# Up products of two feed-forwards as seven block products of 256 tokens in place of eight

## The reference, cut to what matters

```python
# block 1
h = rms_norm(x, ffn_norm)
act = jax.nn.silu(h @ w_gate) * (h @ w_up)
x = x + act @ w_down
# block 2
gate, val = jnp.split(h @ w_up, 2, axis=-1)
x = x + (jax.nn.silu(causal_dwconv(gate, conv_w)) * val) @ w_down
```

## Time and profile before

| | us |
|---|---|
| median of 3 runs | 1906.7 |
| profiled execution | 1906.78 |
| its span in the trace | 1904.9 |
| TensorE busy | 1827.2 |
| VectorE busy | 662.6 |
| ScalarE busy | 698.9 |
| GpSimd busy | 829.2 |

### The profile page before, as it was taken

How to read it: one execution, slowest core, us unless ns; L and a number is a source line. 1 busy time by engine, 2 the same in 40 slices (tenths; PEclk the granted TensorE clock), 3 DMA queues, 4 the chain that set the end, 5 groups by cost and what they waited for, 6 DMA issues and landing times. The chain is left out here.

```text
span 1904.9 us, 23268 instructions
## 1 busy us (share of the span) xinstructions
PE 1827.2 (96%) x9070; PEld 1517.7 (80%) x9070; DVE 662.6 (35%) x1110; ACT 698.9 (37%) x1355; POOL 829.2 (44%) x537
## 2 busy tenths in 40 slices
PE   6999999999999999999989989999998999999998
PEld 5998776778877888888768978887887878888886
DVE  2443333351433110011038438983204233303322
ACT  3233344232333232222236228873423333313322
POOL 2444222234442444444336428982651244444442
PEclk9999999999999999999989989999999999999999
DMA  6232111212352323332324320003441223233331
GB/s 219 78 89 62 47 48 51 56 53 80 98 177 71 95 94 94 100 100 93 107 71 136 102 62 28 1 1 100 133 133 34 67 82 106 90 96 92 104 107 45
DMA packets 222876, 161.87 MB, mean 85 GB/s; under 512 B 9768, under 2 KB 197296, under 8 KB 222768
## 3 DMA queue, kind: packets, MB, share of 16 engines
q1 hardware_dynamic: 221712, 159.32, 28.2%
q10 hardware_dynamic: 1056, 1.06, 0.2%
HBM read 156.15 MB, written 2.11 MB: 83 GB/s over the span
## 5 line engine op out<-in xcount | busy, mean ns | idle before, releaser
L306 POOL TENSOR_TENSOR w_low<-ring,w_high 128x1024 fp32r<-128x1024 f32 (+2 forms) x303 | 682.1, 2257 | 935.6 <-ACT w_high L298 935.6
L319 PE MATMUL psum<-hT,w_high 128*128 128x512 f32 x1232 | 491.8, 399 | 9.8 <-PEq L183 6.1
L321 PE MATMUL psum<-hT,w_low 128*128 128x512 f32 x1232 | 485.0, 394 | 0.0
L320 PE MATMUL psum<-hL,w_high 128*128 128x512 f32 x1232 | 484.9, 394 | 0.0
L298 ACT ACTIVATE w_high<-ring 128x1024 fp32r<-128x1024 f32 (+2 forms) x303 | 296.8, 981 | 507.9 <-PE psum L321 507.8
L319 PEld LDWEIGHTS psum<-hT,w_high 128*128 128x128 f32 x1232 | 235.0, 191 | 63.5 <-issue 11.6
L321 PEld LDWEIGHTS psum<-hT,w_low 128*128 128x128 f32 x1232 | 234.2, 190 | 50.5
L320 PEld LDWEIGHTS psum<-hL,w_high 128*128 128x128 f32 x1232 | 234.9, 191 | 47.1
L319 PE MATMUL psum<-w_high,hT 128*128 128x512 f32 (+2 forms) x384 | 132.9, 346 | 7.2 <-POOL w_low L306 3.3
L319 PE MATMUL psum<-w_high,ffn_act 128*128 128x512 f32 x352 | 139.1, 395 | 0.0
L320 PE MATMUL psum<-w_low,ffn_act 128*128 128x512 f32 x352 | 138.9, 395 | 0.0
(11 more groups left out here) (363 smaller groups left out, 2564.1 us busy)
## 6 DMA issues: line engine op xcount, KB each, us to landing
ring<-in_w_in SPq DMA_DIRECT2D x58, 512.0 KB, 3.8
ring<-in_ffn_w_up SPq DMA_DIRECT2D x44, 512.0 KB, 3.8
ring<-in_w_gate SPq DMA_DIRECT2D x22, 512.0 KB, 3.8
ring<-in_w_up SPq DMA_DIRECT2D x22, 512.0 KB, 3.9
ring<-in_w_down SPq DMA_DIRECT2D x20, 512.0 KB, 3.6
ring<-in_ffn_w_down SPq DMA_DIRECT2D x20, 512.0 KB, 3.7
ring<-in_nsa_w_in SPq DMA_DIRECT2D x18, 512.0 KB, 3.8
ring<-in_ca_wkv SPq DMA_DIRECT2D x16, 512.0 KB, 3.8
```

Source lines behind the costliest of these rows:

```text
L306: nc.gpsimd.tensor_tensor(tile_view(w_low, n, SPLIT), tile_view(ring, n, RING), tile_view(w_high, n, SPLIT), ALU.subtract).then_inc(w_lo, 1)
L319: nc.tensor.matmul(ps, lhsT=sh, rhs=mh, start=first, stop=False)
L320: nc.tensor.matmul(ps, lhsT=sh, rhs=ml_, start=False, stop=False)
L321: return nc.tensor.matmul(ps, lhsT=sl, rhs=mh, start=False, stop=last)
```

## The change

For 40 of the 44 pairs (all but the first two of each feed-forward, `PLAIN` = 2) the pair's product is seen as a 2x2 block matrix A by a 2x2 block matrix B. A11 and A12 are the gate tile's first and last four feature slices, A21 and A22 those of the up tile; B11, B21 are the same feature halves of the first 256 tokens, B12, B22 of the last 256. Seven block products in place of eight give the four quarters of the result, C11, C12 (gate) and C21, C22 (up), by Strassen's scheme in its form with fifteen sums:

S1 = A21 + A22, S2 = S1 - A11, S3 = A11 - A21, S4 = A12 - S2, and T1 to T4 in the same way from B. The products run in the order A11 B11, S2 T2, S1 T1, S3 T3, A12 B21, A22 T4, S4 B22, each of 4 slices x 3 = 12 matmuls of 256 columns. They go to three banks a round (two sets of three alternate); products 4 and 6 overwrite the bank of product 2, so wait for a combination on VectorE (`combined`), as product 7 does for the bank of product 3, and product 5 waits for the copy of product 1's bank (`first_out`).

The four T are made once per feed-forward, high and low, while the two plain pairs run. The four S are made for each pair by VectorE, straight from the ring. The seven operands of weights (512 columns each) rotate over six half places of `w_high` and `w_low`. GpSimd makes six of their low parts, VectorE that of S1. What the first round of u1 needs is prepared in d0 (`ahead`).

```diff
+                        seventh("A11", "B11", a_)
+                        seventh("S2", "T2", b_)
+                        seventh("S1", "T1", c_)
+                        pe.wait_ge(combined, 7 * r + STEPS["U2"])
+                        seventh("S3", "T3", b_)
+                        pe.wait_ge(first_out, r + 1)
+                        seventh("A12", "B21", a_)
+                        pe.wait_ge(combined, 7 * r + STEPS["U3"])
+                        seventh("A22", "T4", b_)
+                        pe.wait_ge(combined, 7 * r + STEPS["U4"])
+                        seventh("S4", "B22", c_, True)
...
+            def add_three(self, v, r):
...
+                nc.vector.tensor_tensor(src("S1"), src("A21"), src("A22"), ALU.add).then_inc(u_sums, 1)
+                nc.vector.tensor_tensor(src("S3"), src("A11"), src("A21"), ALU.subtract).then_inc(u_sums, 1)
+                v.wait_ge(u_sums, 4 * r + SUMS["S1"])
+                nc.vector.tensor_tensor(src("S2"), src("S1"), src("A11"), ALU.subtract).then_inc(u_sums, 1)
...
+            def high(self, a, r, name):
...
+                if i < 6:
+                    a.wait_ge(w_used, run["tile"] - SPLIT + i // 2 + 1)
+                else:
+                    a.wait_ge(u_used, 7 * r + j - 5)
+                nc.scalar.activation(operand_place(w_high, r, j), self.source(r, name), ACT.Copy).then_inc(u_high, 1)
+
+            def low(self, g, r, name):
+                j = OPERANDS.index(name)
+                g.wait_ge(u_high, 7 * r + j + 1)
+                nc.gpsimd.tensor_tensor(operand_place(w_low, r, j), self.source(r, name), operand_place(w_high, r, j),
+                                        ALU.subtract).then_inc(u_low, 1)
```

The program of VectorE, where `conv` are the two taps left to it in block 2 (the first tap is now a scaled copy on ScalarE), `gated` the multiply of silu by the up half, and `low_part` the low part of the result:

```diff
+                    for f in range(FG + 1):
+                        r = seven_of(f)
+                        if plain and f == 0:
+                            token_sums()
+                        if f >= 1 and taps is not None:
+                            conv(f - 1)
+                        if is_seven(f):
...
+                            v.wait_ge(u_used, 7 * r + 2)
+                            v.wait_ge(first_out, r + 1)
...
+                            nc.vector.tensor_tensor(c12, b_, first, ALU.add).then_inc(combined, 1)
+                        if is_seven(f + 1):
+                            seven.add_three(v, r + 1)
+                        if f >= 1:
+                            gated(f - 1)
+                        if is_seven(f):
+                            v.wait_ge(u_used, 7 * r + 4)
...
+                            nc.vector.tensor_tensor(c21, b_, c12, ALU.add).then_inc(combined, 1)
+                            v.wait_ge(combined, 7 * r + STEPS["U3"])
+                            nc.vector.tensor_tensor(c22, c21, c_, ALU.add).then_inc(combined, 1)
+                            nc.vector.tensor_tensor(c12, c12, c_, ALU.add).then_inc(combined, 1)
+                        if is_seven(f + 1):
+                            seven.add_last(v, r + 1)
+                            seven.low_by_vector(v, r + 1)
+                        if f >= 1:
+                            low_part(f - 1)
+                        if is_seven(f):
+                            v.wait_ge(u_used, 7 * r + 5)
+                            nc.vector.tensor_tensor(c11, a_, first, ALU.add).then_inc(combined, 1)
+                            v.wait_ge(u_used, 7 * r + 6)
+                            nc.vector.tensor_tensor(c21, c21, b_, ALU.add).then_inc(combined, 1)
+                            v.wait_ge(u_used, 7 * r + 7)
+                            v.wait_ge(combined, 7 * r + STEPS["U4"])
+                            nc.vector.tensor_tensor(c12, c12, c_, ALU.add).then_inc(combined, 1)
```

More of the change, by code:

```diff
@@ new lines, in token_half, with ffn_stage, seven_of, is_seven @@
+        def token_half(name):
+            i, j = int(name[1]) - 1, int(name[2]) - 1
+            return slice(4 * i, 4 * i + 4), slice(HALF * j, HALF * j + HALF)
+        def ffn_stage(block, name, gate_w, up_w, actT, bufs, taps, f0, plain, r0, sets, ready, vacant):
+            n0 = state["used"]
+            seven, g, sl, val, first, raw_, th, tl, t_sum, t_high, t_low = bufs
+            def seven_of(f):
+                return r0 + f - plain
+            def is_seven(f):
+                return plain <= f < FG
@@ L1756, in high_part @@
                     def high_part(f):
                         a.wait_ge(acted, f + 1)
[L1758 to L1773, removed]
+                        copy(False, actT[0][:, f, :], val[:, f % 2, :]).then_inc(high, 1)
@@ L1774, in _ @@
                         if f >= 1:
                             high_part(f - 1)
-                    high_part(FG - 1)
+                        if more:
+                            seven.high(a, r + 1, "S1")
+                        if f < plain and taps is not None:
+                            a.wait_ge(w_used, n0 + 2 * f + 1)
+                            nc.scalar.activation(g[:, f % 2, 2:], bank[sets[f % 2][0]][:, :], ACT.Copy).then_inc(copied, 1)
+                        if more:
+                            seven.high(a, r + 1, "S3")
+                            seven.high(a, r + 1, "A12")
+                        elif f == FG - 1:
+                            split_high(a, n0 + 2 * FG + 2)
@@ L1810, in _ @@
                 @block.gpsimd
                 def _(g_):
+                    for f in range(FG):
+                        r = seven_of(f)
+                        if is_seven(f):
+                            seven.low(g_, r, "A22")
+                            seven.low(g_, r, "S4")
+                        else:
+                            split_low(g_, n0 + 2 * plain)
+                        if is_seven(f + 1):
+                            for operand in ("A11", "S2", "S3", "A12"):
+                                seven.low(g_, r + 1, operand)
@@ L1835, in after_up, with high_ahead, low_ahead @@
                 def after_up(pe, i):
-                    pe.wait_ge(acted, (8, 8, 9, 9)[i] if i < 4 else FG)
+                    if i >= 2:
+                        pe.wait_ge(acted, FG - 1 if i <= 4 else FG)
+                def high_ahead(a):
+                    for operand in ("A11", "S2", "S1", "S3", "A12"):
+                        seven.high(a, r1, operand)
+                def low_ahead(g_):
+                    for operand in ("A11", "S2", "S3", "A12"):
+                        seven.low(g_, r1, operand)
```

313 lines of the change are left out of this document (264 added, 49 removed).

## The result

The changed kernel takes 1982.93 us (median of 4 runs, 1979.65 to 1986.9), the kernel before 1907.01 beside it: a ratio of 1.0399, 95% interval 1.0379 to 1.042. It is 76 us slower. The forecast was 1972, with a range of 1928 to 2010.

A forecast was written before the change was run, and what follows sets the result against it. TensorE bounds the kernel before; in the changed rounds VectorE and GpSimd, shutting each other out, were to exceed its 9.98 us. 1906.8 us plus 20 x 1.12, 20 x 2.02 and 2 for edges gave 1972, range 1928 to 2010.

The forecast's parts named there:

- TensorE's pace: Up stages: 84 matmuls of 256 columns at 0.1188 us make a round 9.98 us, 0.90 under the old 10.88.
- rival 1: Seven two-input VectorE operations a round: VectorE and GpSimd pass each other, TensorE sets the pace; 1871 us, chance 0.08.
- The exclusion between VectorE and GpSimd: VectorE operations with two SBUF inputs need GpSimd idle and conversely; times add to 10.7 us a round, 11.9 in feed-forward 2.
- The walk for feed-forward 1: One round stepped: ends at 12.55 or 11.5 us by order; middle 12.0 taken, +1.12 us a round.
- unkind order: Feed-forward 1 round: GpSimd's low part of S3 runs before VectorE's low part of S1; the round ends at 12.55 us.
- kinder order: VectorE's low part of S1 gets ahead of GpSimd's S3: rounds of 11.5 us, or 12.4 in feed-forward 2.
- The walk for feed-forward 2: Rounds with taps before the first combination: 13.4 us, or 12.4 in the other order; 12.9 taken, +2.02 us a round.
- The sum: Whole kernel: 1906.8 + 20 x 1.12 + 20 x 2.02 + 2 = 1972 us.
- The edges: Token sums at each feed-forward's start: 21 us against 21.8 of plain pairs; 0 to 4 may show, 1 taken per feed-forward.
- The gapless pair of engines: Rival for the rounds: VectorE and GpSimd full without a gap, 10.7 and 11.9 us; 1926 us, chance 0.15.
- The case in which nothing overlaps: Rival: all VectorE and GpSimd work in a row, 13.7 and 15.2 us a round; 2049 us, chance over 2010 0.11.
- a sagging clock: Part of the nothing-overlaps rival: TensorE's clock sags when less busy, 4% of 500 us is 20 us; shares chance 0.11.

The follow-up runs named there:

- e1: Changed kernel with the second operand of VectorE's four weight sums read from a free PSUM bank (38 of 40 rounds): 1910.26 us, ratio 1.002 to the kernel before.
- e3: Changed kernel with each of GpSimd's six low parts a round replaced by two fills that read no SBUF: 1881.73 us, ratio 0.9872 to the kernel before.
- e7: Version routed through spare PSUM banks with gating product moved later; next round's S1 (S3 too without taps) now also precedes the first combination: 1880.51 us, ratio 0.9861.

## Why the prediction was right, step by step

**TensorE's pace: confirmed.** In a product the matmuls are 0.12 us apart, and where nothing else binds (e1 in feed-forward 1, e3, e7) a round is 9.98 us, the figure of the prediction. With rounds at that pace e7's profiled execution is 1881.2, 10 us above the 1871 worked out for rival 1. Of these some 8 are waits in the first rounds of the up stages (L2102 4.2 and 2.0, L1866 2.2 us in its view of waits). The prediction's 9.2 us a round came from the gap in the Trainium skill ("TensorE: Matmul & The Clock Gate", Back-to-back issue gap); that section gives the formula for a matmul by itself and says that it under-counts at few columns with weight loads. The trace agrees, with 0.119 us a step for the 0.109 estimated from it.

**The exclusion between VectorE and GpSimd: confirmed,** and by taking it away from either side (e1, e3). Rival 1, that they pass each other, falls with it.

**The walk for feed-forward 1: its unkind order held.** The prediction had product 6 start 5.5 us after VectorE's first combination; it does so 5.40 after (656.97 to 662.37). It had TensorE wait 2.1 us there; it waits 1.8. The steady round is 12.43 us, for 12.55 in the walk. First combinations start at 619.15 and, eight rounds on, at 719.81: a mean of 12.58; in the second half 802.51 to 915.22, nine rounds, 12.52. The kinder order never came there: VectorE's low part of S1, where it forks, takes 1.76 us or more in every round of both halves (eight and ten of them, each behind a first combination). Only the first round of the second half, whose operands are made in the down stage, is under 12.1 us: 10.47 (792.04 to 802.51). With it the mean of feed-forward 1 is 12.44.

**The walk for feed-forward 2: both orders occur.** The rows of L1854, VectorE's low part of S1, in two successive rounds of the changed kernel, each with the first combination of its round and the next:

```profile
1809.21 0.41 DVE L2070 TENSOR_TENSOR ffn_g<-psum,ffn_first 128x256 f32<-128x256 f32 x1
...
1814.69 1.78 DVE L1854 TENSOR_TENSOR w_low<-ffn_sums,w_high 128x512 fp32r<-128x512 f32 x1
...
1822.53 0.41 DVE L2070 TENSOR_TENSOR ffn_g<-psum,ffn_first 128x256 f32<-128x256 f32 x1
...
1828.01 0.68 DVE L1854 TENSOR_TENSOR w_low<-ffn_sums,w_high 128x512 fp32r<-128x512 f32 x1
...
1834.96 0.41 DVE L2070 TENSOR_TENSOR ffn_g<-psum,ffn_first 128x256 f32<-128x256 f32 x1
```

Where L1854 waits for GpSimd (1.78) the round is 13.32 us; where it gets ahead (0.68) the round is 12.43. The walk had 13.4 and 12.4, and the same operation at the fork. Of the 17 intervals between first combinations behind the first round, six are of the kind sort, and the mean is 13.0, for the 12.9 taken. Inside the round the walk was less good. It priced both taps as if alone, 0.75 us, but the second meets GpSimd here too:

```profile
1807.43 1.86 DVE L2015 SCALAR_TENSOR_TENSOR ffn_sl<-ffn_g,par,ffn_sl 128x512 f32<-128x512 f32 x1
...
1809.68 0.39 PE L360 MATMUL psum<-ffn_th,w_high 128*128 128x256 f32 x1 [2.41 <-DVE ffn_g L2070]
```

The first combination comes 6.4 us after the start of product 1, for 5.75, and TensorE waits 2.4 us before product 4 and only 0.4 before product 6 (1799.87, and 1813.17 in the next round), where the walk's 5.85 and 10.4 mean 1.6 and 1.7. The combination that frees the bank still ends at 10.3 for 10.4, since S1, S3 and S2 take only 1.43, 0.68 and 0.68 us there. That the round fits so well is in part luck.

**The sum.** With the measured means of the intervals between first combinations, 12.44 and 13.1 us (13.1 counts the slow first round of feed-forward 2, 14.9), it is 20 x (12.44 - 10.88) + 20 x (13.1 - 10.88) = 31.2 + 44.4 = 76 us, and the profiled executions differ by 74.8 (1981.6 against 1906.8). The term most off is the middle taken for feed-forward 1: 12.0 for 12.44, that is 9 us. Feed-forward 2 was 4 us low (12.9 for 13.1), and the edges 2 to 3 us high; together these make the 10 us between 1971.6 and the profiled 1981.6. Averaging two orders was the wrong tool in feed-forward 1, where the schedule repeated the one order that it had fallen into, and it served in feed-forward 2, where both occurred. Each order should have had a time and a chance of its own.

**The edges: overestimated in feed-forward 1.** The sums of tokens take 1.22 us each where nothing contends, as estimated at 1.2:

```profile
598.55 1.22 DVE L2043 TENSOR_TENSOR ffn_quarters<-ffn_quarters 128x1024 f32<-128x1024 f32 x1
```

The stretch from 591.58 to 610 us was worked out as 21 and took 18.4, and TensorE does not wait for it. The 2 us charged for both feed-forwards do not show: the sum above is without them, and already 1 us over the measured difference.

**Rivals.** The gapless pair of engines (1926) was ruled out: the round above takes 12.43 us for 10.7, and GpSimd's rows in it have idle times of 1.38, 1.29 and 0.35 us, each for ScalarE's high part of a sum. The case in which nothing overlaps (2049) was ruled out by the rounds too, 12.4 and 13.1 us for its 13.7 and 15.2. Its milder part, a sagging clock, did occur (0.965 for 0.979), and is told of below.

## What to carry to other kernels

- Before work is given to VectorE or GpSimd, add up over the shortest loop the time in which VectorE reads two SBUF tiles and in which GpSimd reads SBUF. If the sum passes the bounding engine's time, that each of the two would fit alone says nothing.
- Feeding one VectorE operand from a spare PSUM bank turned this change from 4.0% slower to 0.2% faster, and moving the operations still exclusive into VectorE's own waiting time to 1.4% faster. The second step alone, 1979.6 us for 1982.9, gave next to nothing.
- When a walk forks on a small gap, keep both ends, each with a chance, and don't forecast the mean: it held in one feed-forward (13.0 for 12.9) and not in the other (12.4 for 12.0).

## What the runs showed of the hardware that was not expected

**The clock falls after waits of under 2 us, at times.** TensorE's timeline of the changed kernel behind the wait before 674.80 us:

```profile
675.50 0.28 PE L362 MATMUL psum<-ffn_th,w_low 128*128 128x256 f32 x1
675.62 0.37 PE L360 MATMUL psum<-ffn_th,w_high 128*128 128x256 f32 x1
675.78 0.42 PE L361 MATMUL psum<-ffn_tl,w_high 128*128 128x256 f32 x1
676.00 0.42 PE L362 MATMUL psum<-ffn_th,w_low 128*128 128x256 f32 x1
```

and the windows there:

```profile
672.00:674.00 2.00, 0.98 (x9) 0.78 (x7) 2.00 (x3) 0.15 (x1) 1.26 (x1) 1.00 0.47 133
...
676.00:678.00 2.00, 2.00 (x11) 2.00 (x11) 2.00 (x2) 0.75 (x2) 1.47 (x2) 0.50 0.31 77
```

The steps go from 0.12 to 0.21 us for some 16 matmuls: the granted clock is 0.50, which is 1.2 GHz of 2.4. After the wait of 1.81 us before 662.37, one round earlier, there was no such fall. In the window of 619 to 720 us there was one after three of eight waits. In feed-forward 1 a round with a slow stretch takes 12.93 us and the next 12.12, so that three rounds take 37.48 for 3 x 12.43 = 37.29: TensorE does not bind there, and its slow steps are mostly covered. In feed-forward 2 each of the six kind rounds has a slow stretch right behind its first combination, after a wait of 2.4 us, and none of the other eleven behind the first round has one. That the later matmuls are what let VectorE get ahead is likely, but no run tested it. Such steps are most of why TensorE's busy time did not fall with its work: from 619 to 720 us 65 of 668 steps are over 0.17 us without being waits, 14.8 us for the 7.7 of full pace, and this is 0.9 us a round, as much as a round saves. In the other three up stages it is 0.6 to 0.9 us a round. In e7_reordered, where TensorE does not wait, no step from 633 to 700 us is over 0.17 us.

**One SBUF input less on VectorE, or none on GpSimd, ends the exclusion.** A VectorE operation of 128x512 was 0.68 us beside a GpSimd busy for 57 of 70 us as soon as one of its inputs lay in PSUM, and fills on GpSimd cost VectorE nothing, while with full reads by both a turn costs VectorE 1.10 us and GpSimd 0.44 (1.78 for 0.68, 1.73 for 1.29).
